# Weight pieces of four row blocks: half as many stops in the queues of ScalarE and VectorE

## The reference, cut to what matters

```python
z = h @ w_in                       # 1024 x 3840: inputs of four mixers and their gate paths
y_a, y_b, y_c, y_d = conv(z), gqa_attention(z), retention(z), diff_attention(z)
gates = sigmoid(h @ w_mgate)       # 1024 x 4096
merged = sum(gates[i] * ((y_i * silu(gate_i)) @ w_branch[i]) for i in range(4))
x = x + gate * (merged @ w_out)    # 1024 x 1024
```

## Time and profile before

| | |
|---|---|
| median of 3 runs | 1360.62 us (1359.85 to 1360.85) |
| the profiled execution | 1361.9 us, span 1360.1 us |
| TensorE busy | 1327.3 us, 98% of the span |
| VectorE busy | 883.4 us, 65% |
| ScalarE busy | 566.1 us, 42% |
| rounding, L971 | 312 x 623 ns, 181.8 us in all |
| subtraction, L1202 | 312 x 685 ns, 205.7 us in all |
| TensorE's granted clock | 0.999 of full speed over the span |

### The profile page before, as it was taken

One profiled execution on the slowest core, in us unless ns is written; L12 is line 12 of the kernel. 1 busy time (PEld: TensorE's weight loads), 2 busy tenths in 40 slices (PEclk: granted clock), 3 DMA queues, 4 the chain that ended last, 5 costly groups with the idle time before them and its releaser, 6 DMA issues.

```text
span 1360.1 us, 25262 instructions
## 1 busy us (share of the span) xinstructions
PE 1327.3 (98%) x9365; PEld 1252.2 (92%) x9365; DVE 883.4 (65%) x1801; ACT 566.1 (42%) x1252; POOL 78.3 (6%) x99
## 2 busy tenths in 40 slices
PE   5899999999999999999999999999999999999997
PEld 1899999989998999999889999999999999999986
DVE  2587786457666598857875777644866657664455
ACT  1676665234553322213354666532455423222241
POOL 1000000010000000100010000001100000001000
PEclk9999999999999999999999999999999999999999
DMA  9422212123113333355442212122220143214322
GB/s 345 151 62 67 78 40 71 62 60 105 32 33 116 117 110 101 109 170 180 135 158 69 67 40 78 40 63 78 78 71 32 57 147 108 79 40 125 124 78 78
DMA packets 102253, 127.59 MB, mean 94 GB/s; under 512 B 4124, under 2 KB 84600, under 8 KB 102136
## 3 DMA queue, kind: packets, MB, share of 16 engines
q1 hardware_dynamic: 97944, 112.33, 25.6%
q0 software_dynamic: 4192, 13.65, 3.3%
HBM read 119.66 MB, written 6.31 MB: 93 GB/s over the span
## 4 chain that ended last, share of the span: by engine, by line
PE 91%; DVE 4%; ACT 1%; issue 1%; DMA 1%; SPq 0%; POOL 0%; DVEq 0%; ACTq 0%; POOLq 0%
PE G L1582 44%; PE G L1578 14%; PE G L1580 9%; PE BK L1597 8%; PE TO L1698 3%; PE TP L1684 3%; PE S L1675 2%; PE TP L1655 1%; PE TP L1725 1%; PE BK L1612 1%; DMA early_raw<-in_w_ada 1%; PE TP L1643 1%; PE S L1677 1%; PE TO L1717 1%; PE S L1678 1%
## 5 line engine op out<-in xcount | busy, mean ns | idle before, releaser
L1582 PE MATMUL G<-h_hi,w_hi 128*128 128x320 f32 x1472 | 249.8, 312 | 0.0
L1582 PE MATMUL G<-h_hi,w_lo 128*128 128x320 f32 x1472 | 248.7, 311 | 0.0
L1582 PE MATMUL G<-h_lo,w_hi 128*128 128x320 f32 x1472 | 246.6, 310 | 0.0
L1202 DVE TENSOR_TENSOR w_lo<-w_raw,w_hi 128x512 fp32r<-128x512 f32 x312 | 205.7, 685 | 56.8 <-ACT w_hi L971 56.6
L1582 PEld LDWEIGHTS G<-h_lo,w_hi 128*128 128x128 f32 x1472 | 223.0, 188 | 0.0
L1582 PEld LDWEIGHTS G<-h_hi,w_hi 128*128 128x128 f32 x1472 | 221.3, 188 | 1.2 <-issue 0.7
L1582 PEld LDWEIGHTS G<-h_hi,w_lo 128*128 128x128 f32 x1472 | 222.0, 188 | 0.0
L971 ACT ACTIVATE w_hi<-w_raw 128x512 fp32r<-128x512 f32 x312 | 181.8, 623 | 55.4 <-DMA w_raw<-in_w_branch 34.7
L1066 ACT ACTIVATE tg<-G 128x320 f32<-128x320 f32 x128 | 55.6, 435 | 208.9 <-PE G L1582 203.2
L1111 ACT ACTIVATE work<-S,neg_max 128x640 f32<-128x640 f32 (+1 forms) x120 | 85.1, 710 | 124.2 <-DVE neg_max L1394 108.4
L1312 DVE SCALAR_TENSOR_TENSOR tg<-tg,BK 128x320 f32<-128x320 f32 x96 | 46.8, 487 | 112.8 <-PE BK L1597 93.0
(11 more groups left out here) (251 smaller groups left out, 1864.5 us busy)
## 6 DMA issues: line engine op xcount, KB each, us to landing
w_raw<-in_w_mgate SPq DMA_DIRECT2D x32, 1024.0 KB, 5.4
w_raw<-in_w_in SPq DMA_DIRECT2D x29, 1024.0 KB, 5.4
w_raw<-in_w_ada SPq DMA_DIRECT2D x17, 1024.0 KB, 5.1
w_raw<-in_w_branch SPq DMA_DIRECT2D x32, 256.0 KB, 5.6
w_raw<-in_w_out SPq DMA_DIRECT2D x8, 1024.0 KB, 4.9
early_raw<-in_w_ada SPq DMA_DIRECT2D x6, 1024.0 KB, 10.8
work<-gate_rows POOLq DMA_DIRECT2D x4, 512.0 KB, 4.9
za<-in_x_prompt POOLq DMA_DIRECT2D x2, 512.0 KB, 8.2
```

The costliest lines, as they stand in the source:

```text
L1202: V.tensor_tensor(w_lo[:, s.n % 2, a:b, :], raw_rows(s), w_hi[:, s.n % 2, a:b, :].bitcast(F32), ALU.subtract).then_inc(lo_done, 1)
L1582: ins = mm(g[:, 0:HALF], a[:, w, kt, c], b[:, kt, half], start=first, stop=last)
```

## The change

Pieces of all chunks but the first are four row blocks long: two pieces a chunk instead of four, three with a branch (the third is two blocks of `w_branch`). The first chunk, which is loaded in four parts, keeps its four. The gap between pieces is doubled, so that piece i of now stands where piece 2i stood; the branch piece keeps its place. TensorE's waits for a new chunk go by pieces of four row blocks: at block 0 and at block 4.

```diff
     def pieces(c):
-        return [Step("split", l=c.l, n=c.n, part=i, of=c) for i in range(4 if c.branch is None else 5)]
+        return [Step("split", l=c.l, n=c.n, part=i, of=c) for i in range(4 if c.n == 0 else 2 if c.branch is None else 3)]
...
                 for i, piece in enumerate(pieces(nxt[c.n])):
                     piece.k = 1
-                    at = passes + delay + int(gap * i)
+                    at = passes + delay + int(2 * gap * i)
                     due += [(at, piece), (at + 1 * (delay > 1), Step("lowpart", of=piece))]
...
         if k == "split":
-            s.rows = (2 * s.part, 2 * s.part + 2)
+            rows = 4 if s.n else 2
+            s.rows = (rows * s.part, min(rows * (s.part + 1), KT if s.of.branch is None else WK))
...
             s.piece0 = first_piece[new] if new not in chunk_used else None
+            s.piece_rows = 4 if new else 2
...
-                        if s.piece0 is not None and kt in (2, 4, 6) and i != 1:
-                            pe.wait_ge(lo_done if i else hi_done, s.piece0 + kt // 2 + 1)
+                        if s.piece0 is not None and kt and kt % s.piece_rows == 0 and i != 1:
+                            pe.wait_ge(lo_done if i else hi_done, s.piece0 + kt // s.piece_rows + 1)
```

## The result

The changed kernel takes 1365.4 us (median of 6 runs, 1364.93 to 1366.68) against 1360.73 us before (6 runs, 1359.85 to 1361.85): a ratio of 1.0034, 95% interval 1.0024 to 1.0044, so it is slower by 3.3 to 6.0 us. The forecast was 1364.9 us, within 1361.8 to 1367.7.

A forecast was written before the change was run, and what follows sets the result against it. TensorE, busy 98%, was taken as the bound, losing time only where it waits for ScalarE or VectorE. Layer 0's 2.44 and layer 1's 1.90 gave +4.3 us on 1360.62: forecast 1364.9 us, range 1361.8 to 1367.7.

The forecast's parts named there:

- The price of a lone piece: An instruction behind one lone piece comes 0.44 us later on ScalarE, 0.54 us on VectorE, when the piece is long.
- five terms: Layer 0: key groups 0.54, context heads 0.40, tile 1 0.65, 154.81 0.54, 173.16 0.31, together 2.44 us; layer 1: 1.90.
- The choice at 154.81: Layer 0 score group behind a lone VectorE subtraction: +0.54 us taken, 0.30 if it had slack like 134.41.
- 173.16: Layer 0 score group behind a lone ScalarE rounding: +0.31 us taken, between 0.21 and 0.44.
- tile 1: Layer 0, differential queries, score groups at 134.41 and 137.85 held by late exponentials: net +0.65 us; layer 1 the same.
- the give-back: Tile 1 groups at 140.75 and 144.13 stop waiting for the exponential: 0.33 of their 0.42 us taken back.
- The key groups: Layer 0: key split 0.67 us late delays transposes at 83.48; 0.14 comes back; net +0.54 us.
- what I leave at nothing: First uses of chunks at wide units lose, grouped-query heads gain; the two cancel within half a microsecond.
- first uses of chunks: Eighteen at wide units; at most +0.44 us at 705.38. Rival: 0.2 us more each, 3.6 added, about +8 us, chance 0.13.
- the maps of the grouped-query heads: Their transposes wait for a chain starting with TensorE; some pieces there go, so up to 0.5 us back.
- The gain of lighter queues: Rival: half of the 5.9 us of waits at transposes of maps vanish; about -3 us, chance 0.05.
- the first rival: Lateness is paid back at later waits inside a stage; no measurable change, about +1.8 us, chance 0.22.
- second half: If an engine is not saturated but causes bubbles elsewhere, breaking instructions up may finish sooner; so the change goes the wrong way.

The follow-up runs named there:

- pair experiment: Against the kernel before: pieces stay two row blocks long but stand in pairs, back to back, at the places of the long ones; 1365.27 us, ratio 1.0034.

## Why the prediction was right, point by point

**The price of a lone piece**, 0.44 and 0.54 us for what stands behind it, is what the traces show: 0.42 at 137.85 with ScalarE alone changed, 0.54 at 154.81 with both. The pair experiment shows that in these stages it is the time the queue is held.

**The sum by places** held in its five terms: 2.11 us against 2.44 in layer 0, 1.73 against 1.90 in layer 1. The choice at 154.81, 0.54 rather than 0.30, and at 173.16, 0.31 between 0.21 and 0.44, fell on the right side. In tile 1 I was 0.14 us too high: I took the give-back for 0.33 of 0.42, and it was the whole. The key groups, a chain of estimates, came out 0.15 too high: the loss was 0.64 us where 0.67 had been worked out, but 0.25 came back and not 0.14.

**The step that failed** is in "what I leave at nothing": of the first uses of chunks I wrote that "behind them stand only that unit's own matmuls". Behind the subtractions of chunks 14 and 49 on VectorE stands also a normalisation that runs on to a branch unit 17 us later; that cost 0.34 and 0.36 us, in two places I had not named. And behind a rounding stands an evacuation on which the branch unit of 615.41 waits: 0.43 us, which a load shorter by as much hid in this trace. From the maps of the grouped-query heads I hoped for up to 0.5 us and got 0.22. What is left of the two, about +1.0 us with the wide units against the zero assumed, was covered by the five terms being 0.50 too high and by a start-up 0.42 us shorter in this trace. That the size of the forecast is right within 0.5 us is therefore partly luck; that the mechanism and its five places are right is not.

**The rivals.** The gain of lighter queues didn't come: the maps' waits fell from 5.9 to 5.7 us though VectorE and ScalarE were busy for 25 us less. Lateness was paid back inside the stages, but only some 1.8 us of it (0.25 at the key groups, 0.20 and 0.44 in the context heads and tile 1 of each layer, 0.22 at the maps), 1.1 of which the sum had counted; the first rival needed 2.5 more. First uses of chunks cost 0.50 us at two wide units, not 3.6. The rule from the Trainium skill's page "Perfetto Trace Analysis", section "Optimizing Scalar/DVE Operations", went by its second half, as the shares of the earlier trace rows let one expect: eight row blocks are slower than four, four than two. But breaking up alone did not do it: short pieces in pairs held the score groups as long as the long ones. That smaller still would be faster was not tried.

## What to carry to other kernels

In a queue that is not the bound, count neither busy time nor instructions: ask what stands behind each instruction, and whether the bounding engine waits for it; a longer stop there costs its extra length, and a stop that is removed pays only where someone waited. Merging is cheap where nobody waits (57 of 69 chunks here cost 1.2 us) and dear in a few stages (12 chunks, 3.8 us), so it should be decided by stage, and where a piece can go behind the urgent work there is something to win: about 0.45 us at each of three transposes here.

## What the runs showed of the hardware that was not expected

GpSimd's small power instruction is held by VectorE's long subtraction. It ended 1.17 us after the end of the subtraction it overlapped before the change (307.53 + 1.69 = 309.22 against 307.36 + 0.69 = 308.05) and 1.18 us after the long one (311.74 against 310.56): it seems to begin its work when that instruction ends. Its form over 128x4 takes 1.01 us when no such instruction has just begun. Where a subtraction begins 0.17 us ahead of it, it ends 0.87 us after that subtraction. Before (two short subtractions back to back, in one row):

```profile
173.09 1.29 DVE L1202 TENSOR_TENSOR w_lo<-w_raw,w_hi 128x512 fp32r<-128x512 f32 x2
173.26 1.39 POOL L850 TENSOR_TENSOR rs<-st,small 128x4 f32<-128x4 f32 x1 [29.94 <-DVE st L1155]
```

after:

```profile
174.78 1.22 DVE L1204 TENSOR_TENSOR w_lo<-w_raw,w_hi 128x1024 fp32r<-128x1024 f32 x1
174.95 1.92 POOL L852 TENSOR_TENSOR rs<-st,small 128x4 f32<-128x4 f32 x1 [30.79 <-DVE st L1157]
```

and with eight row blocks:

```profile
176.88 2.28 DVE L1208 TENSOR_TENSOR w_lo<-w_raw,w_hi 128x2048 fp32r<-128x2048 f32 x1
177.05 2.98 POOL L856 TENSOR_TENSOR rs<-st,small 128x4 f32<-128x4 f32 x1 [32.72 <-DVE st L1161]
```

From row to row it grows by 0.53 and 1.59 us over the first, as the subtraction grows by 0.53 and 1.60 (685, 1219 and 2285 ns). The second of two short subtractions, which begins while GpSimd's instruction is under way, adds nothing: behind a single short one it takes 1.38 us. The Trainium skill's page "SBUF — State Buffer", section "Who interferes with whom", has the rule: a VectorE instruction with two SBUF inputs contends with a GpSimd instruction that reads SBUF, over a shared pair of ports that it calls an exclusive lock. The traces agree in these rows: the hold lasts until the VectorE instruction ends. What it costs this kernel was not separated. At the branch unit of 319.78 the 0.54 us of GpSimd are made up by the subtraction that fell away; with pairs of short pieces, where the same instruction takes 1.70 us again, that unit starts 0.13 us sooner than before instead of 0.05 later with chunk 14 short.
